# Gate and up of four gated FFNs as seven-product blocks, with their weight sums made by accumulating DMAs

## What is computed

```python
for layer in range(DEPTH):                                   # DEPTH = 2
    x = x + 0.5 * swiglu(rmsnorm(x, norm_ffn1[layer]), ffn1_gate[layer], ffn1_up[layer], ffn1_down[layer])
    x = x + hybrid_mixer(rmsnorm(x, norm_mix[layer]), ...)
    x = x + 0.5 * swiglu(rmsnorm(x, norm_ffn2[layer]), ffn2_gate[layer], ffn2_up[layer], ffn2_down[layer])
return rmsnorm(x, norm_final)
```

## Time and profile before

| | us |
|---|---|
| median of 3 runs | 3690.53 (3685.5 to 3692.14) |
| the profiled execution | 3689.52 |
| its span | 3687.7 |
| PE busy | 3602.9 |
| VectorE busy | 2154.0 |
| ScalarE busy | 1551.4 |
| GpSimd busy | 217.6 |
| mean granted clock | 0.996 |

### The profile page before, as it was taken

The page is one execution under the profiler, slowest core; times in us unless marked ns, Lnnn a source line. Parts: engine busy times, 40 slices in busy tenths (PEclk is TensorE's granted clock), DMA queues, the critical chain, the costliest instruction groups (busy, mean ns, idle before and its releaser), DMA issues.

```text
span 3687.7 us, 46095 instructions
## 1 busy us (share of the span) xinstructions
PE 3602.9 (98%) x17872; PEld 2938.5 (80%) x17872; DVE 2154.0 (58%) x2862; ACT 1551.4 (42%) x2222; POOL 217.6 (6%) x233
## 2 busy tenths in 40 slices
PE   9999899999999999999999999999999999999999
PEld 7777688787678887888877798888888877888887
DVE  4455666666855677435667564356335676564356
ACT  3335344436533444333455443334323464543234
POOL 0001000000200000000000310000000000310000
PEclk9999999999999999999999999999999999999999
DMA  4101256422005663425321014253435321014352
GB/s 183 35 30 40 91 160 190 136 98 92 24 35 183 169 185 115 137 103 171 109 93 49 12 64 137 103 171 109 159 104 162 95 105 49 12 57 156 103 166 91
DMA packets 57384, 394.99 MB, mean 107 GB/s; under 512 B 6480, under 2 KB 6864, under 8 KB 11984
## 3 DMA queue, kind: packets, MB, share of 16 engines
q1 hardware_dynamic: 45072, 303.97, 22.8%
q0 software_dynamic: 12096, 88.09, 10.5%
HBM read 375.26 MB, written 2.10 MB: 102 GB/s over the span
## 4 chain that ended last, share of the span: by engine, by line
PE 83%; DVE 11%; ACT 4%; issue 1%; DMA 0%; DVEq 0%; POOL 0%; SPq 0%; ACTq 0%; POOLq 0%
PE ps L534 81%; DVE split L2247 3%; ACT arena L1282 2%; PE ps L543 2%; DVE X L2251 2%; DVE arena L2251 2%; DVE arena L2247 2%; ACT split L1282 1%; DVE arena L3167 1%; ACT L1282 0%; DVE small L2263 0%; DMA ring<-in_wts 0%; DVE arena L2243 0%; DVE arena L2275 0%; DVE arena L2255 0%
## 5 line engine op out<-in xcount | busy, mean ns | idle before, releaser
L534 PE MATMUL ps<-split 128*128 128x512 f32 (+2 forms) x13260 | 3012.0, 386 | 28.8 <-DVE X L2251 12.3
L534 PEld LDWEIGHTS ps<-split 128*128 128x128 f32 x13260 | 2415.5, 188 | 544.8 <-issue 48.1
L2247 DVE TENSOR_TENSOR split<-ring,split 128x1024 fp32r<-128x1024 f32 x554 | 675.9, 1220 | 859.0 <-ACT split L1282 827.9
L1282 ACT ACTIVATE split<-ring 128x1024 fp32r<-128x1024 f32 x554 | 582.7, 1052 | 1100.8 <-PE ps L534 1053.9
L534 PE MATMUL ps<-arena 128*128 128x128 f32 (+9 forms) x3344 | 486.3, 298 | 23.4 <-ACT arena L1282 8.8
L534 PEld LDWEIGHTS ps<-arena 128*128 128x128 f32 (+2 forms) x3344 | 395.7, 191 | 98.7 <-issue 66.0
L1282 ACT ACTIVATE arena<-ps 128x512 f32<-128x512 f32 (+6 forms) x580 | 297.6, 513 | 341.3 <-PE ps L534 226.7
L2247 DVE TENSOR_TENSOR split<-arena,split 128x1024 fp32r<-128x1024 f32 (+2 forms) x210 | 250.9, 1195 | 92.1 <-ACT split L1282 74.9
L1282 ACT ACTIVATE split<-arena 128x1024 fp32r<-128x1024 f32 (+2 forms) x210 | 217.8, 1037 | 182.1 <-PE ps L534 139.3
L2251 DVE SCALAR_TENSOR_TENSOR X<-ps,X 128x512 f32<-128x512 f32 x252 | 174.3, 692 | 53.7 <-PE ps L534 29.4
L2247 DVE TENSOR_TENSOR arena<-arena 128x512 f32<-128x512 f32 (+6 forms) x246 | 174.3, 708 | 20.0 <-ACT arena L1282 8.5
(11 more groups left out here) (105 smaller groups left out, 1053.7 us busy)
## 6 DMA issues: line engine op xcount, KB each, us to landing
ring<-in_wts SPq DMA_DIRECT2D x268, 1024.0 KB, 4.8
arena<-in_wts POOLq DMA_DIRECT2D x56, 1024.0 KB, 7.9
arena<-arena POOLq DMA_DIRECT2D x14, 1024.0 KB, 10.1
ring<-in_wts POOLq DMA_DIRECT2D x14, 1024.0 KB, 7.9
ring<-in_wts SPq DMA_DIRECT2D x25, 512.0 KB, 3.5
X<-in_x SPq DMA_DIRECT2D x4, 512.0 KB, 5.7
out<-arena SPq DMA_DIRECT2D x4, 512.0 KB, 2.6
ring<-in_wts SPq DMA_DIRECT2D x2, 784.0 KB, 5.7
```

What stands on the lines that cost most here:

```text
L534: return e.matmul(out, l, r, start=start, stop=stop, skip_group_check=True)
L1282: o.sig(a.activation(out, i, f, **kw), sig)
L2247: o.sig(v.tensor_tensor(out, a, b, op), sig)
```

## The change

It replaces the plain groups of gate and up with blocks of the seven-product form, over rows (1024 in two halves of 4 chunks), tokens (two halves of 256) and columns (b11 and b21 are 512 columns of up, b12 and b22 the same 512 of gate). An FFN has five such blocks and a narrow one with 256 + 256 columns. Blocks and down blocks follow each other as gated, gated, down, gated, gated, down, gated, narrow, then the plain groups `fd..20` and `fd..21`.

- The weights stay stationary in a gated block, and a moving chunk has 256 tokens. A product is two pieces (one in the narrow block); each feeds 24 passes.
- The order of the products is now P1, P2, N5, P6, N3, P7, N4 (`ORDER`), for down blocks of these FFNs too. `ONTO` names the products that go on in another's bank after that has been read: N4 goes on in P7's.
- All weight sums of a block stand in ring slots or in one buffer t3: b12 += b11 (`f_one`), t3 = b22, += b12 (`f_base`, `f_t3`), b11 += t3 (`f_t2`), b21 += b11 (`f_t4`), all by DMAs of GpSimd. In the first block of an FFN VectorE makes the first sum (`added_up`), and b11 gets b12 and b22 by two adding DMAs.
- A ring slot is reused in the order in which it comes free. SP's load of the next b12 waits for `f_t4` as well.
- The activations' forms of gate and up are made once for each FFN (`whole`), from raw copies of the transposed tokens; the products of each gated block all use them. Rows 2 and 3 of the tokens are transposed within P1 and P2 of the first block (`between`).
- Forms of a down block's first three products are made in rounds 1, 2 and 6 of the gated block before it.

```diff
+ORDER = (("P1", "b11", "a11"), ("P2", "b21", "a12"), ("N5", "t1", "f5"), ("P6", "t2", "f6"),
+         ("N3", "b22", "f3"), ("P7", "t3", "f7"), ("N4", "t4", "a22"))
+ONTO = {"P6": "P1", "N3": "N5", "P7": "P6", "N4": "P7"}
...
+        ld.slot = slots.pop(0)
+        slots.append(ld.slot)
+        ld.before = held.get(ld.slot)
+        ld.landed = 16 + (ld.before.landed if ld.before else 0)
+        held[ld.slot] = ld
+        return ld
...
+            us.append(B)
+            for q, k0, c0 in (("b11", 0, c1), ("b12", 0, c2), ("b21", h, c1), ("b22", h, c2)):
+                B.loads[q] = load(f"{name}/{q}", key, kbase + k0, h, c0, w)
...
+            for what, b, f in ORDER:
+                ld = B.loads.get({"t1": "b12", "t2": "b11", "t4": "b21"}.get(b, b))
+                of = [piece(ld, q, min(per, h - q), (f"f_{b}", B.count) if b[0] == "t" else None) for q in range(0, h, per)]
...
+            for pc in B.of[2]:
+                summed_up += B.first
...
+            for q, b, added in (("b11", "t2", "f_t4"), ("b12", "t1", None), ("b22", "b22", None), ("b21", "t4", None)):
+                B.loads[q].end, B.loads[q].added = ("lo", end[b]), added and (added, B.count)
+            return B
...
-            quarters = [form(a, 0, 3, up) for a in ("a11", "a21", "a12", "a22")]
-            for c in range(2):
-                row = (f"ghx{l}", f"gm_{l}", 0, 1, 0, 1024) if n_ == 1 else ("nfin", "nfin", 0, 1, 0, 1024) if l else ("gfx11", "g1_1", 0, 1, 0, 1024)
-                lin(f"fd{n_}{l}{p}{c}", f"fd{n_}_{l}", TILES[p], c * 512, 512, False, kbase=8 * p, between=[row] if p + c == 3 else ())
-            lins[f"fd{n_}{l}{p}0"].forms = quarters
-            for pc in lins[f"fd{n_}{l}{p}1"].pieces[-3:]:
-                pc.form = quarters[3].i + 1
-            for f in quarters:
-                f.end = n
+                B = block(f"fd{n_}{l}{p}", f"fd{n_}_{l}", p, 4, 8 * p, 512, 0, 512)
...
+        for r, (what, _, f) in enumerate(ORDER):
+            begun, ps = ONTO.get(what), U.of[r]
+            hi, lo = forms(f)
+            for x in ready(f):
+                e.wait_ge(*x)
+            each = [(t, p) for p in ps for t in range(nt)]
+            for t, p in each:
...
+                if p is ps[0] and begun:
+                    e.wait_ge(*K.read[U.name, begun, t])
+                    of = K.turn[U.name, begun, t]
...
+                    bank(U.name, what, t)
...
+                        at = slice(256 * t + 128 * g, 256 * t + 128 * g + 128)
+                        for k in range(p.c):
+                            kk = p.k + k
+                            i = mm3(b.t[:, 256 * g:256 * g + 256], [v[:, k, at] for v in w], (hi[:, kk, :], lo[:, kk, :]),
+                                    kk + g == 0 and not begun, kk == U.h - 1)
+                else:
+                    at = slice(128 * t, 128 * t + 128)
+                    for k in range(p.c):
+                        kk = p.k + k
+                        i = mm3(b.t[:, :], (hi[:, kk, at], lo[:, kk, at]), [v[:, k, :] for v in w], kk == 0 and not begun, kk == U.h - 1)
+                if t == nt - 1:
+                    i.then_inc(S["used"], 1)
...
+                for t in range(nt):
+                    if U.gated and what != "P7":
+                        early += 1
+                        K.read[U.name, what, t] = (S["early"], early)
+                    else:
+                        partial += 1
+                        K.read[U.name, what, t] = (S["part"], partial)
 
...
 
     def ffn(l, w, J, nxt):
-
...
+        def whole(f):
+            n = {"f5": 1, "f6": 2, "f3": 3, "f7": 4, "a22": 5}.get(f)
+            return [(S["h_form"], begun + n)] if n else [(S["fx_lo"], begun // 5 * 4 + 3 + (f == "a12"))]
+
+        def between(r, q, t):
+            if (r, q, t) in ((0, 1, 0), (1, 0, 0)):
+                J.turned(2 + r)
+        taken["all"] = 0
...
+                block(U, lambda f: shapes[f], lambda f: ())
+            else:
+                own = {f.what: f for f in U.forms}
+                block(U, lambda f: tuple(K.m.formed(own[f])), lambda f: [(S["form"], own[f].i + 1)])
+        Q = quarters(f"fd{w}{l}20")
+        lin(f"fd{w}{l}20", Q, Q.ready, of="side")
+        lin(f"fd{w}{l}21", Q, of="lin", last=nxt.last)
 
...
+        def whole():
+            for x, f in enumerate(("f5", "f6", "f3", "f7", "a22")):
+                a.wait_ge(S["h_sum"], begun * 4 // 5 + min(x, 3) + 1)
+                if x < 3:
+                    a.wait_ge(S["used"], us[0].split_forms[f][1])
+                act(shapes[f][0], F.a22 if f == "a22" else F.a21 if f == "f7" else F.shape, ACT.Copy, "h_hi")
+                yield
+
...
+    def added_up(U, q):
+
+        r = {b: K.RING[:, ld.slot, :] for b, ld in U.loads.items()}
+        for b in ("b11", "b12"):
+            v.wait_ge(S[f"ring{U.loads[b].slot}"], U.loads[b].landed)
+        for p in U.of[2][q:q + 1]:
+            c = slice(p.q * U.w, (p.q + p.c) * U.w)
+            tt(r["b12"][:, c], r["b12"][:, c], r["b11"][:, c], ALU.add, "f_t1")
...
+    def ffn(l, w, own_, name, then):
+        nonlocal side
+        F, us, quarters = K.f, lins[f"ffn{w}{l}"], lins[f"fd{w}{l}20"].forms
+        shapes, begun = F.shapes(us[0]), 5 * (2 * l + w - 1)
+
+        def rows(j):
+            c = slice(128 * (j - 2), 128 * (j - 2) + 128)
+            for g in (0, 1):
+                v.wait_ge(*emptied(own_, j, g))
+            tt(F.shape[:, :, c], F.a21[:, :, c], F.a22[:, :, c], ALU.subtract, "h_sum" if j == 3 else None)
+
+        def whole():
+            for x, (f, more) in enumerate((("f5", (F.shape, F.shape, F.a11, ALU.subtract)), ("f6", (F.shape, F.shape, F.a12, ALU.add)),
+                                           ("f3", (F.a21, F.a11, F.a21, ALU.subtract)), ("f7", None), ("a22", None))):
+                hi, lo = shapes[f]
+                v.wait_ge(S["h_hi"], begun + x + 1)
+                tt(lo, F.a22 if f == "a22" else F.a21 if f == "f7" else F.shape, f32(hi), ALU.subtract, "h_form")
+                if x < 2:
+                    for j in (0, 1):
+                        v.wait_ge(*emptied(own_, j, x))
+                if more:
+                    tt(*more, "h_sum")
+                yield
+
...
+        def two(U):
+            for t in range(U.w // 256):
+                v.wait_ge(*K.read[U.name, "P1", t])
+            took(U, "P2", part, ALU.add)
+
+        def opened(U):
+            for t in range(U.w // 256):
+                v.wait_ge(*K.read[U.name, "P6", t])
+            took(U, "N3", lambda t: at(U, t, 0), ALU.add)
+
+        def closed(U):
+            for t in range(U.w // 256):
+                v.wait_ge(S["silu_u"], 2 * U.done + t + 1)
+                tt(at(U, t, 0), at(U, t, 0), part(t), ALU.mult, "u")
+
+        def last(U):
+            nt = U.w // 256
+            for t in range(nt):
+                v.wait_ge(S["silu_u"], 2 * U.done + nt + t + 1)
+                b = turn[U.name, "N4", t]
...
+        def gate_up(U, D, late):
+
+            wide = U.w == 512
+            for r in range(7):
+                if r == 0:
+                    for _ in late:
+                        pass
+                    if U.first:
+                        rows(2)
+                        split(next(below))
+                        rows(3)
+                        next(extra)
+                        split(next(below))
+                        continue
+                if U.first and r == 1:
+                    next(extra)
+                    continue
+                if r == 2:
+                    two(U)
+                if r == 5:
+                    opened(U)
+                    if wide:
+                        split(next(below))
+                    closed(U)
+                    took(U, "P7", lambda t: at(U, t, 1), ALU.subtract, False)
+                    split(next(below))
+                    next(extra, None)
+                    next(extra, None)
+                else:
+                    split(next(below))
+                    if r == 6:
+                        if D:
+                            form(D.forms[2])
+                    next(extra, None)
+                    if wide:
+                        split(next(below))
+                        next(extra, None)
+                if D and r == 1:
+                    form(D.forms[0])
...
+        def down(U, late):
+
+            _, f7, _, f5, f6, f3, a22 = U.forms
+            q = {a: K.m.quarter(f7, a) for a in ("a11", "a12", "a21", "a22", "sum")}
+            for _ in late:
+                pass
+            stt(q["sum"], q["a21"], -1.0, q["a22"], ALU.mult, ALU.subtract, "shape")
+            tt(q["a11"], q["sum"], q["a11"], ALU.add, "shape")
+            split(next(below))
+            split(next(below))
+            form(f5)
+            read(U, "P1")
+            split(next(below))
+            form(f6)
+            split(next(below))
+            tt(q["a12"], q["sum"], q["a12"], ALU.add, "shape")
+            split(next(below))
```

(65 more changed lines are left out.)

456 lines of the change are left out of this document (317 added, 139 removed).

## The result

The changed kernel takes 3765.6 us in the median (3757.4 to 3770.0, four runs) beside 3691.3 before: ratio 1.020, 95% interval 1.0188 to 1.0212, 74 us slower. The forecast was 3660 and the range ended at 3715, so the prediction was wrong, in its sign too.

The account below looks back on a forecast made before the run. TensorE, busy 98% of 3687.7 us, was taken as the bound. Matmul savings of 69.9 us less waits of 9.6, 4.8, 12 and 12.8 gave 30.7 us gained, so 3660 us; 8-in-10 range 3626 to 3715.

Parts of the forecast that it names:

- The weight sums by DMA: Later blocks: GpSimd's sums for P6 come 1.6 us late behind each of eight down blocks, costing 12.8 us.
- c: Time from issuing f_base through f_t3 to f_t2's landing, ahead of P6; taken as 24.9 us.
- The formula: Waits for the sums: 8 x (c - 23.3) behind down, 8 x (c - 25.4) in down, 8 x (c - 26.4) in other gated blocks, where positive.
- medians in traffic: Median landing times of base copy, t3 add and t2 add beside other DMAs: 6.0 + 11.7 + 10.1 = 27.8 us.
- the sums' chain sets the block's time: Rival: late weight sums decide from c = 27.2 us, costing 66 us at 27.8, against 53 to lose; chance 0.2.
- The first block: Start of each FFN: VectorE's added work makes P6 2.5 us late, the next piece 1.1; 12 us for four FFNs.
- the joins' waits: At the four FFN starts, 0.6 us each in the mean disappears; 1.62 us before the first 256-column pass remains.
- The rival of 112.6 ns: Gated FFN matmuls: weight load hides, a 256-column pass costs half a 512-column one; 3611 us, chance 0.02.
- that of 129 ns: Gated FFN matmuls: 256-column passes at 129 ns make the saving zero; 3715 us, chance 0.02.
- The busy time at full clock: Gate and up matmuls: 1848 passes of 256 columns at 119.6 ns save 17.5 us per FFN, 69.9 for four.
- VectorE's share of the down blocks: VectorE's 37.5 us of work against PE's 37.8 makes splits late: 1.2 us in each of 8 blocks, 9.6 us.
- N4 behind P7: Narrow block: N4 continues in P7's bank and waits for its read-out, 1.2 us for each of four, 4.8 us.

Follow-up runs that it names:

- both sides: Changed kernel with f_one made on VectorE ahead of the splits in wide gated blocks only and the row factors off GpSimd: 3686.2 us, ratio 0.9989.

## Why the prediction was wrong, step by step

**The chain of sums** is the step that failed: the term "The weight sums by DMA" took c = 6.0 + 11.7 + 7.2 = 24.9 us and 12.8 us of waits. Its c was too low. Over the eight blocks behind down blocks the trace of after has c = 27.9 to 30.6, 29.2 in the mean. The formula gives 8 x (29.2 - 23.3) = 47 us, the timeline 49.1. In the other eight gated blocks c is 27.2 to 29.3, and once 34.5; the excess over 26.4, block by block, adds up to 17.4 us, and 17.4 were measured. For these two places the formula held. In the down blocks it asked for too much: c of 25.8 to 28.5 against the 25.4 allowed would cost 9.9 us, and 2.4 were measured, at the two blocks where c was largest. So 68.9 us stand where 12.8 were predicted, 56.1 more; 5.7 of them are the first FFN's second block, which the row factors made late.

The 4.3 us that c lacked, in the mean of the eight blocks behind down blocks, have three sources: `f_t2` 9.2 us instead of 7.2, the t3 add 13.1 instead of 11.7, and 1.0 us between landings and issues, which the sum did not have. In the block followed above they are 11.0, 13.0 and 0.8 us. There `f_t2` met SP's load of the next b11, issued 0.35 us before it; this is the link that the prediction took to run "nearly alone". Where no such load meets it the median is 6.9, in the run with b11's load later. The trace of before had this spread: its SBUF adds that landed in 7.2 and 7.3 us had an SP load beside them for 2.3 and 2.4 us of that time, and the two that took 11.9 had one for 8.3 and 10.5 us.

I had the medians in traffic, 27.8, in hand, and took the lower row for the last link. The rival "the sums' chain sets the block's time" was the right one; it had 0.2. At its 27.8 us it gave 66 us of waits. But with its own terms (53 - 66) it would still have ended near 3703 and not at 3766, since it had no term for the clock either.

**The clock** was not in the sum at all. The loss is 34.7 us larger than before, and 22.4 of that go with the sums. The trace of after has, placed one by one, ten falls to 0.50 at waits of the chain (the eight behind down blocks, and those of 7.69 and 3.19 us), 21.4 us of loss, and six at the beginnings of the FFNs (behind waits of 2.5 to 8.2 us), 12.2 us. The run without sums has the second kind alone, again 12.2. In the run with nine long waits filled 12 us of loss were gone. The trace of before could not show it inside an FFN, as its PE never waited there that long. Here a missing wait was not only mis-sized; it brought a second price with it.

**The first block.** 12 us were taken for four FFNs, and 27.0 measured at the beginnings and around them. The wait itself was foretold well: P6 is 2.34 to 2.70 us late in all FFNs of the run without sums, where the prediction had 2.5; the piece behind it 0.8 where it is seen (1.1 predicted) and N3 0.3 to 0.5 (nothing predicted). Two things were missing. In the first FFN GpSimd's adds for b11 stood behind the row factors, which are not in the prediction's list of what the queue holds: 8.18 us in place of 2.36, and the second block's wait besides, together 7.0 us of the time by the run that moves them. And at the joins PE waits 7.8 us more than before, ahead of transposes (3.54, 3.56 and 1.70 us) and of the last FFN's first pass (4.49), where the prediction had the joins' waits gone but for 1.62. What VectorE and ScalarE do in these joins was not followed.

**What held.** A 256-column pass takes 118 ns with the DMA engines at 0.77, and 120.0 over a whole gated block of the run without sums (336 in 40.3 us); predicted 119.6. The rival of 112.6 ns and that of 129 ns are both out. The busy time at full clock fell by 59.7 us in after and 63.8 without the sums, not 69.9. The shortfall, 10.2 and 6.1 us, is about what the down blocks add: in the run without sums their 168 passes take 38.8 us besides the wait ahead of P2, where 37.8 stood before, 1.0 us more for each of eight. The pass count is the same; why they take longer was not found. VectorE's share of the down blocks was 9.6, measured 6.1, and at another place (ahead of P2, not N5); it is busy for 34.5 of 39 us there, as foretold. N4 behind P7 was 4.8, measured 3.5. The matmul count was exact.

**The balance**, from the predicted span of 3657.0 us: +56.1 chain, +15.0 beginnings, -4.8 VectorE and N4, +34.7 clock, +10.2 matmuls = 3768.2.

Three things stay open: the joins' added waits, the longer down blocks, and whether `f_one` delays the t3 add by its place in the queue or by its share of the engines.

## What to carry over

Where a chain of DMAs fed by a freed buffer must land inside one block, add up its links at their loaded times, and add the gap between landing and next issue for each; the loaded sum is the forecast, and the unloaded one the rival. List every instruction in the issuing queue, DMAs of other purposes and small arithmetic too, since one add issued ahead of the t3 add cost 78 us here. And a wait of several microseconds on an otherwise dense TensorE is to be priced above its length: the ten waits of 3 to 8 us on the chain cost 21 us of clock here beside their 60 us of length.

## What the runs showed of the hardware

- An adding DMA of 1 MB from HBM (`f_t3`) lands in 12.8 us (median) with another add issued 5.5 us before it, and in 9.0 us without that one. An SBUF-to-SBUF add took 6.9 us where no load met it and up to 11.0 beside a load of 1 MB.
- After a stall of 7.56 us the clock was 0.50 for the first 2.5 us of work and 0.71 over the next two; 24 passes began in 4.5 us where the full clock needs 2.9. After 1.9 us of waiting it was down in one place (0.59) and full in another.
- Moving VectorE's sum of 2.5 us for each wide gated block from ahead of the first splits to behind them cost 34.7 us over the kernel (3720.9 against 3686.2 in the run "both sides"), with VectorE busy for 67 and 68% of the span: what counted was the place in its queue and who waits for it.
